# A bias table built in the pooling stage, and a recurrence that multiplies two operands at once

## What is computed

```python
def band_bias_and_mask(rel_bias, n_blocks):
    d = q + BLOCK - s                      # q in 0..127, s in 0..255
    in_window = (d >= 0) & (d < WINDOW)
    bias = rel_bias[t5_bucket(jnp.maximum(d, 0))]      # [H, 128, 256]
    ...
def sliding_window_attention(...):
    logits = logits + bias; logits = where(valid, logits, -inf)
    ...
def _rwkv7_scan(r, w, k, v, a, b):         # a = -kk, b = kk * ah
    def step(S, inp):
        sa = einsum('bhij,bhj->bhi', S, a_t)
        S = S * w_t[:, :, None, :] + sa[..., None] * b_t[:, :, None, :] + v_t[..., None] * k_t[:, :, None, :]
        y = einsum('bhij,bhj->bhi', S, r_t)
        return S, y
```

## Time and profile before

| | us |
|---|---|
| median of 3 runs | 2924.72 (2914.51 to 2925.63) |
| the profiled execution | 2931.59 |
| its span | 2929.9 |
| PE busy in it | 2671.8 |
| DVE busy in it | 1240.8 |
| ACT busy in it | 782.9 |
| granted PE clock, mean | 0.959 |

### The profile page before, as it was taken

How to read it: one execution, slowest core, us unless ns; L and a number is a source line. 1 busy time by engine, 2 the same in 40 slices (tenths; PEclk the granted TensorE clock), 3 DMA queues, 4 the chain that set the end, 5 groups by cost and what they waited for, 6 DMA issues and landing times. The chain is left out here.

```text
span 2929.9 us, 48958 instructions
## 1 busy us (share of the span) xinstructions
PE 2671.8 (91%) x20693; PEld 2222.0 (76%) x20693; DVE 1240.8 (42%) x2037; ACT 782.9 (27%) x1479; POOL 287.1 (10%) x190
## 2 busy tenths in 40 slices
PE   9799999999997699888999999999799998777776
PEld 8799999999986566667888888887677776776455
DVE  5433333333343358452333333333534553444447
ACT  6311111111143149432121111111221412223221
POOL 2100000000011015120000000001400000222102
PEclk9899999999998899998999999999899998999878
DMA  3211111111035600222111111112312112000032
GB/s 139 87 44 44 43 48 54 48 43 43 29 108 129 199 30 2 94 101 86 44 43 60 47 43 43 43 44 86 122 44 77 41 65 95 4 4 4 4 122 101
DMA packets 63100, 183.66 MB, mean 63 GB/s; under 512 B 10470, under 2 KB 19847, under 8 KB 61519
## 3 DMA queue, kind: packets, MB, share of 16 engines
q1 hardware_dynamic: 62928, 181.18, 18.7%
HBM read 150.54 MB, written 30.03 MB: 62 GB/s over the span
## 5 line engine op out<-in xcount | busy, mean ns | idle before, releaser
L790 PE MATMUL f0gu<-b1XH,f0w0H 128*128 128x346 f32 (+1 forms) x528 | 170.4, 323 | 7.0 <-DVE f0w0L L722 6.3
L742 DVE TENSOR_TENSOR f1hf<-f1sg,f1gu 128x512 f32<-128x512 f32 x44 | 30.3, 688 | 337.7 <-ACT f1sg L689 337.7
L742 DVE TENSOR_TENSOR f0hf<-f0sg,f0gu 128x346 f32<-128x346 f32 (+1 forms) x66 | 34.1, 516 | 326.6 <-ACT f0sg L689 326.6
L753 DVE TENSOR_TENSOR Y<-f0dn,Y 128x512 f32<-128x512 f32 (+1 forms) x180 | 124.0, 689 | 113.6 <-PE f0dn L837 112.7
L792 PE MATMUL f0gu<-b1XH,f0w0L 128*128 128x346 f32 (+1 forms) x528 | 170.5, 323 | 0.0
L791 PE MATMUL f0gu<-b1XL,f0w0H 128*128 128x346 f32 (+1 forms) x528 | 169.9, 322 | 0.0
L792 PE MATMUL f0gu<-b1XH,f0w1L 128*128 128x346 f32 (+1 forms) x528 | 169.7, 321 | 0.0
L790 PE MATMUL f0gu<-b1XH,f0w1H 128*128 128x346 f32 (+1 forms) x528 | 169.4, 321 | 0.0
L791 PE MATMUL f0gu<-b1XL,f0w1H 128*128 128x346 f32 (+1 forms) x528 | 169.0, 320 | 0.0
L753 DVE TENSOR_TENSOR Y<-f1dn,Y 128x512 f32<-128x512 f32 x160 | 109.2, 689 | 90.7 <-PE f1dn L837 90.7
L790 PE MATMUL f1gu<-b1XH,f1w0H 128*128 128x512 f32 x352 | 139.4, 396 | 6.3 <-DVE f1w0L L722 6.3
(11 more groups left out here) (402 smaller groups left out, 6588.2 us busy)
## 6 DMA issues: line engine op xcount, KB each, us to landing
f0raw<-in_w_gate_up SPq DMA_DIRECT2D x43, 512.0 KB, 5.7
f1raw<-in_w_gate_up SPq DMA_DIRECT2D x43, 512.0 KB, 5.6
residual<-Y SPq DMA_DIRECT2D x32, 512.0 KB, 2.8
Y<-in_w_ada SPq DMA_DIRECT2D x8, 1536.0 KB, 6.7
f0rawd<-in_w_down SPq DMA_DIRECT2D x22, 512.0 KB, 3.3
f1rawd<-in_w_down SPq DMA_DIRECT2D x22, 512.0 KB, 3.3
w_in_b_raw<-in_w_in_b SPq DMA_DIRECT2D x16, 512.0 KB, 3.3
w_in_a_raw<-in_w_in SPq DMA_DIRECT2D x11, 512.0 KB, 4.7
```

The lines of the kernel that those rows point to most:

```text
L742: dve.tensor_tensor(hf[:, i, 0:w], sg[:, i, 0:w], gu[:, i, 1, 0:w], ALU.mult).then_inc(s["mul"], 1)
L753: dve.tensor_tensor(y, dn[0:r, (par * ND + i) % 4], y, ALU.add).then_inc(s["acc"], 1)
L790: pe.matmul(o, wH[c][:, j, k], xh, start=(k == 0), stop=False)
```

## The change

Three things are done.

1. The bias table is made in the pooling stage by a new class `BiasTable`: the inputs are loaded behind the first six tiles, the product stands on PE behind the bands of tile 1 (its result in `pool_tp`, which is free then), the copy on DVE at the end of step k = 1, and the write is cut into eight pieces of 16 copies of all heads, one behind the store of each of the tiles 0 to 7. `BiasGuest` keeps the read, in four pieces of four heads at m = 5 to 8.
2. In the recurrence `both` multiplies ab, or k, with r and kk in one product of 128 columns (`PB[rows(e), c:c + 13:12, ...]` picks r's and kk's column blocks), so that `inner` and `keys` each are 16 such products. Eight products of 64 columns (`inner_odd`) remain, for the odd row half in the other place. The step rbk and the function `reads` are gone: DVE masks the r parts as "rb" and "rk" right behind the kk parts, into three slots of `RBK`. `rt` is made at h = 2 instead of 5, and `inner` waits for it.
3. The load of the gates moves from the recurrence to `recurrent_output`, last of its loads.

```diff
+        bias.begin(ctx, tp[0:HEADS, 0:3].rearrange("p f t -> p (f t)"))
...
                 load(5)
+                bias.sync_inputs(sp)
                 for t in range(N):
                     if t + XS < N:
                         load(t + XS)
                     keep(t)
+                    bias.sync_table(sp, t)
                 sp.wait_ge(s["stored"], 16 * N)
+                bias.sync_end(sp)
...
+class BiasTable:
+    COPIES = 16
+    def sync_table(self, sp, t):
+        if t < P // self.COPIES:
+            if t == 0:
+                sp.wait_ge(self.s_ge, 1)
+            rows = self.g[:, :].rearrange("h (o w) -> h o w", o=1).broadcast_to([HEADS, self.COPIES, self.W])
+            sp.dma_start(self.table[:, self.COPIES * t:self.COPIES * (t + 1)], rows).then_inc(self.s_out, 16)
...
 class BiasGuest(Guest):
-        if m == 3:
-            sp.wait_ge(self.s_ge, 1)
-            sp.dma_start(table, self.g[:, :].rearrange("h (o w) -> h o w", o=1).broadcast_to([HEADS, P, self.W])).then_inc(self.s_out, 16)
-        if m == 7:
-            sp.wait_ge(self.s_out, 16)
+        if 5 <= m < 5 + HEADS // self.PART:
+            h = self.PART * (m - 5)
...
+            sp.dma_start(self.bias_rows[:, h:h + self.PART, :], skew).then_inc(self.s_read, 16)
```

```diff
@@ DVE
                 def masked(t):
                     pa.wait(dve, t, "ab")
-                    po.wait(dve, t - 2, f"u{LV - 1}")
-                    da.mark(dve.tensor_tensor(LT[:, t % 2], natural(), wide(trix), ALU.mult), "lt")
                     pw.wait(dve, t - 2, "uu")
-                    da.mark(dve.tensor_tensor(turned(t), wk[...], wide(lvl[0]), ALU.mult), "xm")
+                    for e in range(2):
+                        da.mark(dve.tensor_tensor(turned(t)[:, :, e]..., parts(1)[:, :, e], m, ALU.mult), "xm" if e else "xm0")
+                    po.wait(dve, t - 2, f"u{LV - 1}")
+                    half(t, 0, "lt")
+                    pd.wait(dve, t - 3, "y1")
+                    read(t, 0, "rb")
+                def odd(t):
+                    pa.wait(dve, t, "ab1")
+                    half(t, 1, "lt1")
                 def keys(t):
...
+                    read(t, 1, "rk")
-                def reads(t):
-                    pd.wait(dve, t, "rbk")
-                    pd.wait(dve, t - 1, "y1")
...
@@ PE
-                def gram(left, right, t, e, c, q, place, part):
-                    o = 4 * H * part + H * c
-                    return pe.matmul(wk[place, e, o:o + H], left[rows(e), c, chunk(t, q)], right[rows(e), c, chunk(t, q)], start=True, stop=True)
+                def both(left, t, e, c, q):
+                    pair = PB[rows(e), c:c + 13:12, chunk(t, q)]
+                    return pe.matmul(wk[at(e, q), e, 2 * H * c:2 * H * (c + 1)], left[rows(e), c, chunk(t, q)], pair, start=True, stop=True)
                 def inner(t):
-                    da.wait(pe, t, "bt")
+                    da.wait(pe, t, "rt")
...
+                def inner_odd(t):
+                    da.wait(pe, t, "rb")
+                    for c in range(4):
+                        for q in range(2):
+                            mm = pe.matmul(wk[rows(q), 1, H * c:H * (c + 1)], ab[rows(1), c, chunk(t, q)], kk[rows(1), c, chunk(t, q)], start=True, stop=True)
                 def keys(t):
-                    da.wait(pe, t, "kt")
+                    da.wait(pe, t, "lt1")
-                steps = {..., 4: ("st0", "rbk"), ...}
+                steps = {..., 4: ("st0",), ...}
...
                             if h == 3:
                                 inner(t + 1)
+                            if h == 4:
+                                inner_odd(t + 1)
```

174 lines of the change are left out of this document (95 added, 79 removed).

## The result

| | before | after |
|---|---|---|
| median of four runs each, us | 2922.53 (2914.51 to 2925.63) | 2883.18 (2879.69 to 2888.51) |
| ratio | | 0.9864 [0.9847, 0.9880] |
| profiled execution, us (span) | 2931.59 (2929.9) | 2883.58 (2881.9) |

A second set of runs beside the kernel before gave 0.9881 [0.9864, 0.9897], 34.5 us.

What follows compares the result with a forecast made beforehand. PE, busy 91% of the span, was taken to bound the kernel, so gains come only where it waits or runs below full rate. Terms -27 + 0 - 13.5 + 4.5 = -36 us gave 2889 us, range 2875 to 2908.

Steps and rivals of the forecast that it cites:

- The write of the table held the next w_q load: Projection: the load, issued behind the table's 34.3 us write, came late, giving PE waits of 15.9 and 6.9 us.
- Rivals 2 and 3: Projection: 2, DVE and SP's loop takes over, 18.5 instead of 27, 2897 (0.12); 3, load late anyway, 2916 (0.05).
- Size of the projection term, -27: Projection of layer 1: both PE waits and the slow clock go, minus 27 us, bounds 18.5 and 28.
- The loop of DVE and SP falls behind by about 1.1 us a part: Projection: loop of 12.4 to 12.8 us against PE's 11.2 to 11.5; 8 us in hand, five parts use 5.5.
- Pooling zero: Pooling stage: making and writing the table there costs nothing; plus 34 us if every piece were exposed.
- Rival 4: Pooling stage: the write's eight pieces stall it, eight times 4.3 us, giving 2923 us; chance 0.05.
- Recurrence, fewer instructions: -13.5: Recurrence: 128 instructions fewer a tile, half a block, save 2.0 us a round of supply; minus 13.5 us, bounds 0 and 16.
- rival 1: Recurrence: supply is not the limit, holes are a fee of about 1 us per block; 13.5 becomes about 3, 2899; chance 0.15.
- 4.0 us per block: Recurrence: time PE takes per 256 instructions, from tiles of 32.9 us with 8.25 blocks each.
- 128-column products go side by side: Recurrence: four quadrants run at once, 0.055 us a product, 1.8 us for 32, so PE's own time stays.
- rival 5: Recurrence: 128-column products run one after another at 0.22 us, 42 us in all, giving 2944 us; chance 0.03.
- New order on DVE: +4.5: Recurrence: halved masks lengthen tile 0's start from 5.6 to 9.8 us; plus 4.5 us, bounds 2 and 8.

Runs made afterwards that it cites:

- e2_rec: Kernel before with only the recurrence's part and the move of the gates' load, bias table as before: 2913.77 us, ratio 0.9952.
- e4_no_rbk: Kernel before with 31 of the 32 read-step products left out, so y is wrong: 2914.03 us, timed once.
- e10_split: Changed kernel with each 128-column product made as two of 64 again from the third tile on: 2899.35 us, ratio 0.9909.
- e3_narrow: Changed kernel with every recurrence product but the decay sums narrowed to 16 of 64 columns from the third round, masks and state decay zero: 2931.54 us.
- e6_both_narrow: Changed kernel with zero masks and state decay, only the 32 merged products a tile narrowed to 2 x 16 columns from the third round: 2883.69 us.
- e1_table: Kernel before with the bias table's part only, recurrence and gates as before: 2901.57 us, ratio 0.9916.
- e11_after_again: The changed kernel run once more, unaltered, as base for the runs beside it: 2891.33 us, ratio to before 0.9881.
- e8_late: Changed kernel with the table's product moved behind the first tile's mixing products and its copy one tile later: 2887.85 us, ratio 0.9869.
- e7_start: Changed kernel with tile 0's odd half and k products in the inverse's empty banks, PE waiting for the first read mask: 2879.82 us, ratio 0.9847.

## Why the prediction was right

- **The write of the table held the next w_q load.** Right. With it gone DVE's wait of 31.58 us is gone, the waits are 3.3 to 6.6 us, and PE's 15.9 and 6.9 us with them. Rivals 2 and 3 fall: no wait for the V copy stayed, and no first part was late.
- **Size of the projection term, -27.** 29.7 in the mean of the profiles: 158.4, 158.0 and 158.6 before, 128.3, 128.9, 128.8 and 128.4 with the change. The term began at 964.6 us, and the two parts behind that gave the 27.7 of that sum (50.8 us before, 23.0 now). The rest lay ahead of the first hole. From the stage's start to the second evacuation of QT it was 43.7 us in the profile before (909.44 to 953.17) and is 41.9 now (907.67 to 949.58). That is not the change's doing: with the old projection e2_rec and e4_no_rbk had 42.3 and 42.5 there. But the first hole ended 71.0 to 71.2 us after the stage's start in all three, with PE waiting 15.9, 17.3 and 17.2 us, so the load set that time and PE's pace ahead of it did not matter. The profile that the forecast was read from has the shortest of the three waits. The quarter reads cost nothing, as forecast (8.1 us to land, no wait of PE).
- **The loop of DVE and SP falls behind by about 1.1 us a part.** Right in kind, near in size: 12.0 to 12.7 us a part against PE's 11.1 to 11.5.
- **Pooling zero.** The failed term, hidden by the two kinds of start. The prediction said "PE asks after the second tile's sums, at 23": that time came from a profile of the slow kind, where the two inputs are there in time. In the quick kind PE asks at 19.2, waits 2.0 us and makes the product at half clock in 1.46 us; the cost is 3.4 us. Rival 4 (the pieces) falls.
- **Recurrence, fewer instructions: -13.5.** The mechanism is right and rival 1 wrong: e10_split brings 2.3 us a round back with hardly more work, e3_narrow has no holes where a block's work takes 4.7 us, and e6_both_narrow saves work and no time. In size 2.0 us a round was forecast; the profiles with the changed recurrence give 30.2 in the mean (148.8, 153.3, 153.8, 149.5, 148.8 over five rounds), those with the old one 32.6: 2.4. The step "4.0 us per block" was a little high (3.7 to 3.9), so half a block should give 1.9; the 0.4 to 0.5 us that e10_split and the means show beyond it are not explained. With the last part of the stage the term measures 15.5 us in the means (five rounds 12.1, the rest 3.4), and 17.6 in e4_no_rbk.
- **128-column products go side by side.** Right: 192 products in 15.1 us of PE's time, 0.079 us each, more than the 0.055 estimated and far from the 0.22 of rival 5. That 0.22 was itself misread: the 1.77 us of the earlier trace rows fell mostly into a stretch in which the granted clock was 0.50 (2576.5 to 2579.9); the same 16 records take 1.16 us in the earlier trace rows, 0.145 us a product. At that price rival 5 would have given about 2925, no change, and not 2944.
- **New order on DVE: +4.5.** Right as the sum has it: 4.6 at the first products of the inverse (8.9 us behind the first product of ab, where about 10 were expected), 4.8 at the third round (47.0 to 48.1 against 42.4 and 43.2). But by then two rounds have had fewer instructions, which gave 2.2 us in e4_no_rbk, so the order alone costs about 7. The terms -13.5 and +4.5 were each too small, and the errors took each other away: -9.0 forecast, -10.7 in the means. The clock has no part in it: it rose 27.0 us after the first sums in both kernels.
- **Gates zero.** Nothing speaks against it. From the recurrence's end to the output projection it takes 61.6 to 65.5 us in the three profiles with the old place of the load and 61.3 to 65.7 in the others, so the +1.1 of the table is within what one kernel does.
- **Sum.** -29.7 + 3.4 (or 0.5 in a slow start) - 10.7 = about -37 to -40, and 34.5 to 39.4 were measured. The forecast of -36 had the errors of projection and pooling, and of the recurrence's two terms, against each other: the mechanisms were right, that the sum came so near is in part luck.

Left open: why the same recurrence takes from 266 to 276 us in different executions (its holes range from 32 to 38 us), and why PE's clock rises at 9 us in one execution and at 17 in another. The late rise also goes with a later feed-forward: it was 101 us where the clock, once up, fell again for 3.4 us (before, e1_table, e11_after_again), and 103.4 and 104.9 us where it fell for 6.8 and 10.2 us (e8_late, e7_start).

## What to carry to other kernels

A long write on the queue that also feeds the weights costs what its followers lose, so look for the load behind it, and move it to a stage whose queue is idle; hold the landing of its inputs against the earliest time at which the engine can ask, not against one profile. Where a trace shows PE idle "for issue" every 127 or so f32 products' records, count instructions: merging two products that share a weight saves their supply even when no column is saved. One profile of a stage is one draw: with a spread of 10 us in a stage, take the mean of several before a term is called mis-sized.

## What the runs showed of the hardware

- Fewer columns made the same products slower: with 16 columns instead of 64 the granted clock went to 0.50 and the recurrence from 265.9 to 316.8 us; zeros among the operands did nothing to the clock (1.00).
- PE got its instructions in blocks at one per 3.8 us, with every hole a multiple of about 127 MATMUL records from the one before: 2.5 us from a block's packet to PE's going on and 1.3 us from there to the next packet. Where PE's own work takes 4.7 us a block, the holes are gone (none after 2521.2 us in e3_narrow).
- An early wait can cost its clock too: 4.4 us less waiting at the recurrence's start gave 7.6 us by the third round, the granted clock being 0.98 instead of 0.50 in the 5 us that followed. An equally short way to the inverse in the kernel before, with PE busy for 5.4 of the first 10 us instead of 6.7, kept 0.50 for 27 us.
- An execution began with PE at the lower pace, one record of a 128x512 f32 product every 0.85 us, up to 8.3 to 9.4 us in nine profiles and up to 16.3 to 17.4 us in five, and every 0.43 us from there on; the profile's windows show 1.00 for both, because its clock records begin with the rise.
